# Attention values computed transposed in a hybrid decoder trunk on one core

## The chip, the core and the metric

The kernel runs on one core of one Trainium2 chip. The metric is the device time of one execution in microseconds (us); a comparison takes the median of several executions. The engines work in parallel, each through its own queue in order, and wait for each other through semaphores: TensorE (PE: matrix products, with weight loads PEld beside them), VectorE (DVE), ScalarE (ACT), GpSimd (POOL) and SyncE (SP), which here only issues transfers.

## What is computed

One layer on 256 tokens of width 1024, all in float32:

```
h = rmsnorm(x, g_mix);  proj = h @ w_in           # q, k, v (8 heads of 64), u, gate_a, gate_c
o = causal_softmax(q k^T / 8) v                   # one block of 256 keys: plain causal attention
branch_a = sigmoid(gate_a) * (o @ w_attn_up)
z = u_a * sigmoid(u_g);  z = causal depthwise conv(z, 31 taps) + b_dw
branch_c = sigmoid(gate_c) * (silu(layernorm(z)) @ w_conv_pw + b_conv_pw)
x = x + (branch_a + branch_c) @ w_out
x = x + relu(rmsnorm(x, g_ffn) @ w_ff1)^2 @ w_ff2
out = rmsnorm(x, g_final)
```

## The kernel before

**Products.** Weights arrive in units of 512 x 512 (1 MB). A unit goes through one of four slots: SP loads it into `raw`, ACT casts it to a high part `w_hi` (`high(n)`), DVE subtracts to get the low part `w_lo` (`low(n)`), and PE makes, for 2 token tiles and 4 row chunks, three products: high weights with low activations, high with high, low with high (`products`, L797), 24 in all, each 512 columns wide. The low and high parts of unit n + 3 are made while unit n runs (`AHEAD`). Units 0 to 17 are `w_in`, 18 and 19 `w_attn_up`, 20 and 21 `w_conv_pw`, then `w_out` and the MLP, which ends in a loop.

**Order.** Everything is written out by hand: one loop `for n in range(...)` per engine, in which the step of unit n is followed by what else the engine does "in slot n". Semaphores tie the engines.

**Attention.** Four pairs p of two heads. In slot 9 + p PE makes the scores of pair p (`scores`, L854), for the second 128 queries against 256 keys and for the first 128 against 128 keys, and adds the causal mask by a product of the identity with `mask_b`, as wide as the scores. The scores go to banks 6 and 7 (`SB0`), one bank per head. DVE takes the row maxima (`row_max`), ACT the exponentials with their row sums (`exps`) into `probs`. In slot 10 + p PE transposes the six 128 x 128 blocks (`probs_transposed`) into banks 4 and 5 (`TB`), and ACT copies them to `probs_t` (`probs_out`). In slot 11 + p PE multiplies them, as stationary operand, with the value rows (`values`), 64 columns per product, into columns 384 to 511 of the score banks; DVE multiplies by the inverse row sums (`inverse`, `o_out`) into `o_nat`. The order on PE in a slot is: unit, values, transposes, scores; and `scores(p)` waits for `o_out(p - 2)` (`o_made`). In slot 15 (`S_OT`) PE transposes `o_nat` by eight blocks, ACT and DVE split the result into `b_hi` and `b_lo`, the operand of unit 18.

**Beside it.** DVE makes the convolution in slots 2 to 14 (`conv_products`), one instruction of 256 columns per tap and channel chunk, 124 in all; `CONV_AT` says how many in which slot. ACT evicts every pair of units from PSUM (`take`), with a sigmoid for the gates; a change between Exp and Sigmoid costs a table load. In slot 13 (`S_BIAS`) it casts the bias rows, from which POOL takes the low part.

Of the kernel before, what the change touches and what calls it, by code (L numbers as in the profile page):

```python
# [48 lines left out]
S_OT = S_ATT + 6  # L49
# [5 lines left out]
CONV = [(tap, c) for tap in range(10) for c in (0, 1)]  # L55
CONV += [(tap, c) for tap in range(10) for c in (2, 3)]
CONV += [(tap, c) for tap in range(10, TAPS) for c in range(4)]
CONV_AT = {2: 6, 3: 14, 4: 9, 5: 9, 6: 9, 7: 9, 8: 9, 9: 10, 10: 10, 11: 10, 12: 10, 13: 10, 14: 9}
assert len(CONV) == sum(CONV_AT.values()) == TAPS * 4

# [18 lines left out]
def conv_before(m):  # L79

    tap, c = CONV[m]
    return CONV.index((tap - 1, c))


def build(nc, x, g_mix, w_in, b_glu, w_dw, b_dw, ln_g, ln_b, w_conv_pw, b_conv_pw,
# [35 lines left out]
    with ExitStack() as ctx:  # L121
# [23 lines left out]
        o_nat = sb("o_nat", [P, TT, A])  # L145
# [27 lines left out]
        gmix_rows = o_nat[0:KD, 0, 2 * P:3 * P]  # L173
        vec_rows = o_nat[0:VROWS, 0, 0:P]
        dw_rows = o_nat[0:TAPS * CC, 1, 0:P]
# [13 lines left out]
        def tile_chunks(bank, t):  # L189

            return ps[:, bank + t, :].rearrange("p (c t) -> p c t", c=4)

# [32 lines left out]
        z_made = sem("z_made")  # L225
        conv_step = sem("conv_step")
# [19 lines left out]
        o_made = sem("o_made")  # L246
        o_tr = sem("o_tr")
# [37 lines left out]
        def _(sp):  # L285
# [16 lines left out]
            for n in range(1, U_LOOP):  # L302
                if n // 2 <= UG:
                    load_halves(n, slice(0, HK), raw_full[n])
                else:
                    load(n, unit_source(n))
                if n == 1:
                    for row, v in ((V_BGLU, b_glu), (V_BDW, b_dw), (V_LNG, ln_g), (V_LNB, ln_b), (V_GFFN, g_ffn)):
                        rows = v.shape[1] // P
                        sp.dma_start(o_nat[row:row + rows, 0, 0:P], v.rearrange("l (c p) -> (l c) p", p=P)).then_inc(vec_full, 16)  # L310
# [65 lines left out]
        def _(act):  # L376
# [63 lines left out]

            def probs_out(p):
# [6 lines left out]
            for n in range(U_LOOP):  # L448
# [6 lines left out]
                if n in GLU_AT:  # L455
                    act.wait_ge(vec_made, 1)
                    for c in (2 * GLU_AT[n], 2 * GLU_AT[n] + 1):
                        act.wait_ge(glu_tr, c + 1)
                        nc.scalar.activation(conv[:, c], ps[:, TB + c, T:2 * T], ACT.Sigmoid,
                                             bias=vec[:, V_BGLU + CC + c:V_BGLU + CC + c + 1]).then_inc(glu_sig, 1)  # L460
                if n == S_QT:
                    qk_out(0, TB)
# [5 lines left out]
                if n < U_ATTN and n % 2 == 1 and n // 2 < GA:  # L468
                    take(n // 2)
                if S_ATT + 1 <= n <= S_ATT + PAIRS:  # L470
                    probs_out(n - S_ATT - 1)
                if S_ATT <= n < S_ATT + PAIRS:
                    exps(n - S_ATT)
                if n == S_ATT + PAIRS - 1:
# [3 lines left out]
                if n == S_OT:  # L478
                    act.wait_ge(o_tr, 1)
                    nc.scalar.copy(b_hi[:, 0:CC], chunks(TB)).then_inc(o_hi, 1)  # L480
# [73 lines left out]
        def _(dve):  # L554
# [31 lines left out]
            def conv_products(step):  # L586

                for m in conv_share(step):
                    tap, c = CONV[m]
                    if tap == 0:  # L590
                        nc.vector.tensor_scalar(conv[:, c], z[:, c, 0:T], dw[:, c:c + 1], vec[:, V_BDW + c:V_BDW + c + 1],
                                                ALU.mult, ALU.add).then_inc(conv_step, 1)
                    else:
                        dve.wait_ge(conv_step, conv_before(m) + 1)
                        w = tap * CC + c
                        nc.vector.scalar_tensor_tensor(out=conv[:, c], in0=z[:, c, tap:tap + T], scalar=dw[:, w:w + 1],  # L596
                                                       in1=conv[:, c], op0=ALU.mult, op1=ALU.add).then_inc(conv_step, 1)
# [14 lines left out]

            def o_out(p):

                dve.wait_ge(pv_done, p + 1)
                dve.wait_ge(rinv_made, p + 1)
                for s in range(2):
                    last = nc.vector.tensor_tensor(
                        o_nat[:, 1 - s, 128 * p:128 * p + 128].rearrange("p (h d) -> p h d", h=2),
                        ps[:, SB0:SB0 + 2, 384 + HD * s:384 + HD * s + HD],  # L620
                        rinv[:, p, 2 * s:2 * s + 2].rearrange("p (h a) -> p h a", a=1).to_broadcast([P, 2, HD]), ALU.mult)
                last.then_inc(o_made, 1)
# [8 lines left out]
            for n in range(U_LOOP):  # L631
# [10 lines left out]
                if S_ATT + 2 <= n < S_ATT + 2 + PAIRS:  # L642
                    o_out(n - S_ATT - 2)
                if S_ATT + 1 <= n < S_ATT + 1 + PAIRS:
                    inverse(n - S_ATT - 1)
                if S_ATT <= n < S_ATT + PAIRS:
                    row_max(n - S_ATT)
                if n == S_OT:
                    dve.wait_ge(o_hi, 1)
                    nc.vector.tensor_tensor(b_lo[:, 0:CC], chunks(TB), b_hi[:, 0:CC].bitcast(F32),  # L650
                                            ALU.subtract).then_inc(o_lo, 1)
# [81 lines left out]
                if n + AHEAD < U_LOOP + AHEAD_LOOP:  # L733
                    low(n + AHEAD)
                conv_products(n)

# [49 lines left out]
        def _(pe):  # L786
# [67 lines left out]
            def scores(p):  # L854

                if p >= 2:
                    pe.wait_ge(o_made, p - 1)
                for s, at, keys in ((1, 0, 256), (0, 256, 128)):  # L860
# [4 lines left out]
                    for h in range(2):  # L865
                        last = nc.tensor.matmul(ps[:, SB0 + h, at:at + keys], ident_b[:], mask_b[:, T - keys:T],  # L866
# [3 lines left out]
            def probs_transposed(p):  # L870
                pe.wait_ge(exp_made, p + 1)
                if p:
                    pe.wait_ge(pt_made, p)
                for blk in range(6):
                    o = blk * P
                    last = transpose(ps[:, TB + o // W, o % W:o % W + P], probs[:, o:o + P])
                last.then_inc(p_tr, 1)

            def values(p):

                pe.wait_ge(pt_made, p + 1)
                if p:
                    pe.wait_ge(o_made, p)
                if p + 2 <= PAIRS:
                    pe.wait_ge(exp_made, p + 2)
                for s in range(2):
                    for h in range(2):
                        head = slice(HD * (2 * p + h), HD * (2 * p + h) + HD)
                        o = 384 + HD * s
                        n_keys = 2 - s  # L890
                        for kb in range(n_keys):
                            at = 256 * h + P * kb if s == 0 else 512 + P * h
                            last = nc.tensor.matmul(ps[:, SB0 + h, o:o + HD], probs_t[:, at:at + P], v_nat[:, kb, head],  # L893
                                                    start=kb == 0, stop=kb == n_keys - 1)
# [12 lines left out]
            for n in range(1, U_ATTN):  # L907
# [22 lines left out]
                if S_ATT + 1 <= n <= S_ATT + PAIRS:  # L930
                    probs_transposed(n - S_ATT - 1)
                if S_ATT <= n < S_ATT + PAIRS:
                    if n == S_ATT:
                        pe.wait_ge(qk_made, 2)
                        pe.wait_ge(ident_made, 3)
                    scores(n - S_ATT)
                if n == S_OT:
                    pe.wait_ge(o_made, PAIRS)
                    transpose_chunks(TB, lambda t, c: o_nat[:, t, c * P:c * P + P]).then_inc(o_tr, 1)
                if n == S_LN:  # L940

                    pe.wait_ge(conv_step, TAPS * CC)
                    pe.wait_ge(o_lo, 1)
# [125 lines left out]
```

## Time and profile before

| | us |
|---|---|
| median of 3 executions | 367.96 |
| lowest, highest | 367.62, 368.09 |
| the profiled execution | 368.44 |
| its span, first to last instruction | 366.5 |
| PE busy in the span | 355.6 (97%) |
| DVE, ACT, POOL busy | 245.8, 174.9, 9.2 |

The profile is one execution of the same program. Durations of PE's matmuls overlap, since they are pipelined: what one costs in a stream is the distance between two starts, not its own length. In a timeline, consecutive instructions of a kind are one row with their count; an fp32 product is recorded as two passes, so that six products are x12. In brackets stand an engine's idle time before an instruction and the instruction that released it.

### The profile page before, as it was taken

The page shows a single profiled execution, that of the slowest core. Times are in us where ns is not written, and L with a number is a line of the kernel's source. Part 1 is how long each engine was busy: PE and PEld are TensorE (multiplying, and loading weights), DVE is VectorE, ACT ScalarE, POOL GpSimd, SP SyncE. Part 2 cuts the span into 40 slices and gives each one's busy share as a digit, 9 for nine tenths or more (in the row PEclk, how much of TensorE's full clock was granted, in tenths as well). Part 3 has the DMA queues.
Part 4 walks back from the last instruction along what each step waited for, and adds up shares of the span by engine and source line. Part 5 has one row for each costly group of instructions (what it writes and reads, how often), then busy time and mean ns, then how long its engine had stood idle before and what let it go on. Part 6 is the DMA issues. An engine that isn't in the chain of part 4 may idle for free.

```text
span 366.5 us, 5099 instructions
## 1 busy us (share of the span) xinstructions
PE 355.6 (97%) x2019; PEld 306.7 (84%) x2020; DVE 245.8 (67%) x298; ACT 174.9 (48%) x195; POOL 9.2 (3%) x18
## 2 busy tenths in 40 slices
PE   6999999999999999999999999999999999999993
PEld 3778888777788888888999899898998989989882
DVE  1779999898899779983837561736626375362734
ACT  3694454564493555353635643436344263541513
POOL 3000000000021000000000000000000000000000
PEclk9899999999999999999999999999999999999998
DMA  8998465533334563756364493671837628360003
GB/s 274 348 341 309 120 224 156 190 116 114 116 114 119 196 236 104 257 190 219 116 220 127 128 324 121 201 256 32 313 114 220 238 73 274 111 229 0 0 0 114
DMA packets 33993, 63.71 MB, mean 174 GB/s; under 512 B 1178, under 2 KB 5434, under 8 KB 33980
## 3 DMA queue, kind: packets, MB, share of 16 engines
q1 hardware_dynamic: 33676, 63.01, 51.7%
q10 hardware_dynamic: 304, 0.53, 0.4%
q8 instruction: 9, 0.15, 0.2%
q14 instruction: 4, 0.03, 0.0%
HBM read 62.48 MB, written 1.05 MB: 173 GB/s over the span
## 4 chain that ended last, share of the span: by engine, by line
PE 90%; DVE 5%; issue 2%; DMA 2%; ACT 0%; SPq 0%; POOLq 0%; POOL 0%
PE ps L805 20%; PE ps L801 20%; PE ps L802 19%; PE ps L1001 8%; PE ps L1002 8%; PE ps L1003 8%; PE ps L788 3%; DVE conv L596 2%; DMA raw<-in_w_in_dram 2%; DVE w_lo L558 1%; PE ps L863 1%; PE ps L893 1%; PE ps L866 1%; DVE smax L602 0%; DVE w_lo L575 0%
## 5 line engine op out<-in xcount | busy, mean ns | idle before, releaser
L801 PE MATMUL ps<-w_hi,a_lo 128*128 128x512 f32 x288 | 114.3, 397 | 2.5 <-DVE a_lo L570 2.5
L805 PE MATMUL ps<-w_lo,a_hi 128*128 128x512 f32 x288 | 113.0, 392 | 0.3 <-DVE w_lo L575 0.3
L802 PE MATMUL ps<-w_hi,a_hi 128*128 128x512 f32 x288 | 112.8, 392 | 0.0
L1001 PE MATMUL ps<-b_lo,w_hi 128*128 128x256 f32 x256 | 72.6, 284 | 0.0
L1002 PE MATMUL ps<-b_hi,w_hi 128*128 128x256 f32 x256 | 72.4, 283 | 0.0
L1003 PE MATMUL ps<-b_hi,w_lo 128*128 128x256 f32 x256 | 72.4, 283 | 0.0
L385 ACT CAST w_hi<-raw 128x2048 fp32r<-128x2048 f32 (+1 forms) x30 | 56.4, 1884 | 30.8 <-PE ps L805 26.5
L754 DVE TENSOR_TENSOR w_lo<-raw,w_hi 128x2048 fp32r<-128x2048 f32 x28 | 63.5, 2290 | 11.1 <-ACT w_hi L532 11.1
L558 DVE TENSOR_TENSOR w_lo<-raw,w_hi 128x2048 fp32r<-128x2048 f32 x29 | 66.0, 2282 | 5.1 <-ACT w_hi L385 5.0
L801 PEld LDWEIGHTS ps<-w_hi,a_lo 128*128 128x128 f32 x288 | 54.6, 190 | 13.3 <-DVE w_hi L564 2.7
L805 PEld LDWEIGHTS ps<-w_lo,a_hi 128*128 128x128 f32 x288 | 54.4, 189 | 12.3 <-DVE w_lo L575 0.8
L802 PEld LDWEIGHTS ps<-w_hi,a_hi 128*128 128x128 f32 x288 | 54.6, 190 | 10.6
L532 ACT CAST w_hi<-raw 128x2048 fp32r<-128x2048 f32 x28 | 52.7, 1910 | 7.5 <-PE ps L805 7.5
L596 DVE SCALAR_TENSOR_TENSOR conv<-z,dw,conv 128x256 f32<-128x256 f32 x120 | 50.7, 492 | 0.0
L1001 PEld LDWEIGHTS ps<-b_lo,w_hi 128*128 128x128 f32 x256 | 49.1, 192 | 0.6 <-ACT nat L516 0.3
L1002 PEld LDWEIGHTS ps<-b_hi,w_hi 128*128 128x128 f32 x256 | 49.1, 192 | 0.3
L1003 PEld LDWEIGHTS ps<-b_hi,w_lo 128*128 128x128 f32 x256 | 49.1, 192 | 0.0
L741 DVE TENSOR_TENSOR nat<-nat 128x1024 f32<-128x1024 f32 x7 | 8.6, 1225 | 46.4 <-ACT nat L516 46.4
L516 ACT ACTIVATE nat<-ps 128x512 f32<-128x512 f32 x16 | 9.6, 598 | 60.4 <-PE ps L1003 60.4
L801 PE MATMUL ps<-w_hi,b_lo 128*128 128x512 f32 x48 | 18.9, 393 | 0.0
L805 PE MATMUL ps<-w_lo,b_hi 128*128 128x512 f32 x48 | 18.7, 390 | 0.0
L802 PE MATMUL ps<-w_hi,b_hi 128*128 128x512 f32 x48 | 18.7, 389 | 0.0
(113 smaller groups left out, 227.1 us busy)
## 6 DMA issues: line engine op xcount, KB each, us to landing
raw<-in_w_ff_dram SPq DMA_DIRECT2D x32, 1024.0 KB, 5.5
raw<-in_w_in_dram SPq DMA_DIRECT2D x14, 1024.0 KB, 5.2
raw<-in_w_out_dram SPq DMA_DIRECT2D x4, 1024.0 KB, 5.1
raw<-in_w_in_dram SPq DMA_DIRECT2D x6, 512.0 KB, 7.8
raw<-in_w_attn_up_dram SPq DMA_DIRECT2D x2, 1024.0 KB, 5.0
raw<-in_w_conv_pw_dram SPq DMA_DIRECT2D x2, 1024.0 KB, 5.0
res<-in_x_dram SPq DMA_DIRECT2D x2, 512.0 KB, 3.8
raw<-in_w_in_dram SPq DMA_DIRECT2D x4, 256.0 KB, 5.6
```

The costliest lines, as they stand in the source:

```text
L385: nc.scalar.copy(w_hi[:, n % SLOTS, part], raw[:, n % SLOTS, part]).then_inc(hi_made, 1)
L532: nc.scalar.copy(w_hi[:, slot], raw[:, slot]).then_inc(hi_made, 1)
L558: nc.vector.tensor_tensor(w_lo[:, n % SLOTS], raw[:, n % SLOTS], w_hi[:, n % SLOTS].bitcast(F32), ALU.subtract).then_inc(lo_made, 1)
L596: nc.vector.scalar_tensor_tensor(out=conv[:, c], in0=z[:, c, tap:tap + T], scalar=dw[:, w:w + 1], in1=conv[:, c], op0=ALU.mult, op1=ALU.ad ...
L754: nc.vector.tensor_tensor(w_lo[:, slot], raw[:, slot], w_hi[:, slot].bitcast(F32), ALU.subtract).then_inc(lo_made, 1)
L788: return nc.tensor.transpose(dst, src, ident[0:src.shape[0], 0:src.shape[0]])
L801: nc.tensor.matmul(dst, lo[:, tok], w_hi[:, slot, k], start=start, stop=False)
L802: nc.tensor.matmul(dst, hi[:, tok], w_hi[:, slot, k], start=False, stop=False)
L805: return nc.tensor.matmul(dst, hi[:, tok], w_lo[:, slot, k], start=False, stop=stop)
L1001: nc.tensor.matmul(dst, w_hi[:, slot, k, cols], b_lo[:, kk], start=kk == 0, stop=False)
L1002: nc.tensor.matmul(dst, w_hi[:, slot, k, cols], b_hi[:, kk], start=False, stop=False)
L1003: last = nc.tensor.matmul(dst, w_lo[:, slot, k, cols], b_hi[:, kk], start=False, stop=kk == KD - 1)
```

## The change

Value rows become the stationary operand and the transposed probabilities move. The product then comes out transposed, so that the output transposes of slot 15 are gone. The inverse row sums can no longer be applied to the output (they would run along its columns), so ACT scales `probs` before they are transposed (`normalise`). In detail:

- `values(p)`: four products with 64 stationary columns, of 256, 256, 128 and 128 moving columns; the two heads write the lower and the upper 64 partitions of one piece of bank 5 (`o_pair`).
- `o_out(p)` moves from DVE to ACT, as a copy of 256 columns to `o_t`, in ACT's slot 11 + p ahead of `probs_out`.
- `scores(p)` comes ahead of `probs_transposed(p - 1)` in a slot and waits for `exp_made` of the pair before.
- `probs_transposed(p)` waits for `norm_made` and for `ot_made` of the pair before.
- `inverse(p)` moves a slot earlier on DVE, behind `low(n + 3)`.
- The masks are 128 columns wide throughout.
- Tap 0 of the convolution, with the bias, moves to ACT in slots 2 and 4; DVE is left with 120 instructions.

```
             def normalise(p):
+                act.wait_ge(rinv_made, p + 1)
+                act.wait_ge(exp_made, p + 1)
+                for h in range(2):
+                    part = probs[:, 256 * h:256 * h + 256]
+                    nc.scalar.activation(part, part, ACT.Copy, scale=rinv[:, p, h:h + 1])
+                for h in range(2):
+                    part = probs[:, 512 + 128 * h:640 + 128 * h]
+                    last = nc.scalar.activation(part, part, ACT.Copy, scale=rinv[:, p, 2 + h:3 + h])
+                last.then_inc(norm_made, 1)
+            def o_out(p):
+                act.wait_ge(pv_done, p + 1)
+                nc.scalar.copy(o_t[:, p], o_pair()).then_inc(ot_made, 1)
...
+                    for c in (2 * GLU_AT[n], 2 * GLU_AT[n] + 1):
+                        act.wait_ge(z_made, c + 1)
+                        nc.scalar.activation(conv[:, c], z[:, c, 0:T], ACT.Identity, scale=dw[:, c:c + 1],
+                                             bias=vec[:, V_BDW + c:V_BDW + c + 1]).then_inc(conv_first, 1)
...
             def scores(p):
-                if p >= 2:
-                    pe.wait_ge(o_made, p - 1)
...
-                        last = nc.tensor.matmul(ps[:, SB0 + h, at:at + keys], ident_b[:], mask_b[:, T - keys:T],
+                        last = nc.tensor.matmul(ps[:, SB0 + h, at + keys - P:at + keys], ident_b[:], mask_b[:, P:T],
                                                 start=False, stop=True)
             def probs_transposed(p):
-                pe.wait_ge(exp_made, p + 1)
+                pe.wait_ge(norm_made, p + 1)
                 if p:
                     pe.wait_ge(pt_made, p)
+                    pe.wait_ge(ot_made, p)
...
             def values(p):
                 pe.wait_ge(pt_made, p + 1)
                 if p:
-                    pe.wait_ge(o_made, p)
-                if p + 2 <= PAIRS:
-                    pe.wait_ge(exp_made, p + 2)
+                    pe.wait_ge(ot_made, p)
+                for kb in range(2):
                     for h in range(2):
                         head = slice(HD * (2 * p + h), HD * (2 * p + h) + HD)
+                        at = 3 * h * P + 2 * P * kb
+                        last = nc.tensor.matmul(o_pair()[HD * h:HD * h + HD, kb * P:T], v_nat[:, kb, head],
+                                                probs_t[:, at:at + T - kb * P], start=kb == 0, stop=kb == 1)
```

PE, slot 11, between the last product of unit 11 and the first of unit 12. `v_nat` and `probs_t` are values and transposed probabilities, `qk_t` the queries and keys. Before:

```order
L805 MATMUL ps<-w_lo,a_hi 128x512
L893 MATMUL ps<-v_nat,probs_t 128x64 x6
L788 MATMUL ps<-ident,probs 128x128 x6
L863 MATMUL ps<-qk_t 128x256 x2
L866 MATMUL ps<-mask_b,ident_b 128x256 x2
L863 MATMUL ps<-qk_t 128x128 x2
L866 MATMUL ps<-mask_b,ident_b 128x128 x2
L801 MATMUL ps<-w_hi,a_lo 128x512
```

Now:

```order
L822 MATMUL ps<-w_lo,a_hi 128x512
L903 MATMUL ps<-probs_t,v_nat 64x256 x2
L903 MATMUL ps<-probs_t,v_nat 64x128 x2
L876 MATMUL ps<-qk_t 128x256 x2
L879 MATMUL ps<-mask_b,ident_b 128x128 x2
L876 MATMUL ps<-qk_t 128x128 x2
L879 MATMUL ps<-mask_b,ident_b 128x128 x2
L805 MATMUL ps<-ident,probs 128x128 x6
L818 MATMUL ps<-w_hi,a_lo 128x512
```

The transposes of the probabilities have moved behind the scores, and the values are four products instead of six.

PE, slot 13, where there are no scores any more; the brackets name what an instruction waits for. Now:

```order
L822 MATMUL ps<-w_lo,a_hi 128x512
L903 MATMUL ps<-probs_t,v_nat 64x256 [waits ot_made,pt_made]
L903 MATMUL ps<-probs_t,v_nat 64x256
L903 MATMUL ps<-probs_t,v_nat 64x128 x2
L805 MATMUL ps<-ident,probs 128x128 [waits ot_made,pt_made,norm_made]
L805 MATMUL ps<-ident,probs 128x128 x5
L818 MATMUL ps<-w_hi,a_lo 128x512 [waits lo_made,hi_made,evac]
```

The transposes stand straight behind the values, and wait for ACT's copy of these values' result; before, they waited for `pt_made` and `exp_made`.

ACT, from the end of slot 12 into slot 13: exponentials of pair 3, a table load with the gates of unit pair 5, the high part of unit 16, the bias rows. Before:

```order
L446 COPY probs_t<-ps 128x768
L433 ACTIVATE probs,psums<-ps,nbias 128x256 x2
L436 ACTIVATE probs,psums<-ps,nbias 128x128 x2
L422 ACT_TABLE_LOAD
L422 ACTIVATE gates<-ps,rstd 128x512 x2
L385 CAST w_hi<-raw 128x2048
L467 CAST bias_rows<-gfin_bc 128x1024
L446 COPY probs_t<-ps 128x768
L422 ACTIVATE gates<-ps,rstd 128x512 x2
```

Now:

```order
L468 COPY probs_t<-ps 128x768
L438 ACTIVATE probs,psums<-ps,nbias 128x256 x2
L441 ACTIVATE probs,psums<-ps,nbias 128x128 x2
L452 ACTIVATE probs<-probs,rinv 128x256 x2
L455 ACTIVATE probs<-probs,rinv 128x128 x2
L427 ACT_TABLE_LOAD
L427 ACTIVATE gates<-ps,rstd 128x512 x2
L390 CAST w_hi<-raw 128x2048
L495 CAST bias_rows<-gfin_bc 128x1024
L461 COPY o_t<-ps 128x256
L468 COPY probs_t<-ps 128x768
L427 ACTIVATE gates<-ps,rstd 128x512 x2
```

The four scalings (L452, L455) stand behind the exponentials, and the copy of the output (L461) behind the bias cast.

## Rows read from the trace of the kernel before

**Rows 1.** The page's first part, and the head of its fourth, by engine.

```profile
PE 355.6 (97%) x2019; PEld 306.7 (84%) x2020; DVE 245.8 (67%) x298; ACT 174.9 (48%) x195; POOL 9.2 (3%) x18
...
PE 90%; DVE 5%; issue 2%; DMA 2%; ACT 0%; SPq 0%; POOLq 0%; POOL 0%
```

**Rows 2.** Timeline of PE, slots 10 and 11: start, us, engine, line, tiles.

```profile
77.39 0.82 PE L788 MATMUL ps<-ident,probs 128*128 128x128 f32 x6
78.13 0.70 PE L863 MATMUL ps<-qk_t 64*128 64x256 f32 x4
...
86.45 0.82 PE L788 MATMUL ps<-ident,probs 128*128 128x128 f32 x6
87.67 0.70 PE L863 MATMUL ps<-qk_t 64*128 64x256 f32 x4 [0.39 <-DVE o_nat L618]
88.30 0.39 PE L866 MATMUL ps<-mask_b,ident_b 128*128 128x256 bf16 x2
88.62 0.49 PE L863 MATMUL ps<-qk_t 64*128 64x128 f32 x4
89.05 0.29 PE L866 MATMUL ps<-mask_b,ident_b 128*128 128x128 bf16 x2
```

**Rows 3.** Timeline of PE, slots 12 to 15.

```profile
98.68 0.48 PE L801 MATMUL ps<-w_hi,a_lo 128*128 128x512 f32 x1
...
104.22 1.45 PE L893 MATMUL ps<-v_nat,probs_t 128*128 128x64 f32 x12
105.50 0.83 PE L788 MATMUL ps<-ident,probs 128*128 128x128 f32 x6
...
118.47 1.04 PE L788 MATMUL ps<-ident,o_nat 128*128 128x128 f32 x8
119.26 0.47 PE L801 MATMUL ps<-w_hi,a_lo 128*128 128x512 f32 x1
```

**Rows 4.** Groups by line and shape: busy us, mean ns of one.

```profile
L397 ACT ACTIVATE a_hi<-ps,gmix 128x256 fp32r<-128x256 f32 x8 | 3.1, 474 | 1.1 <-PE ps L788 1.1
```

**Rows 5.** Timeline of DVE, slot 12.

```profile
98.91 0.69 DVE L602 TENSOR_REDUCE smax<-ps 128x2 f32<-128x512 f32 x1 [1.68 <-PE ps L866]
...
99.96 0.17 DVE L607 TENSOR_SCALAR nbias<-smax 128x4 f32<-128x4 f32 x1
100.04 2.28 DVE L558 TENSOR_TENSOR w_lo<-raw,w_hi 128x2048 fp32r<-128x2048 f32 x1
102.24 4.04 DVE L596 SCALAR_TENSOR_TENSOR conv<-z,dw,conv 128x256 f32<-128x256 f32 x10
```

**Rows 6.** Timeline of ACT, slots 12 and 13.

```profile
100.17 0.48 ACT L433 ACTIVATE probs<-ps,nbias 128x256 f32<-128x256 f32 x1 [2.54 <-DVE nbias L607]
100.54 0.19 ACT L433 ACTIVATION_READ_ACCUMULATOR probs<-ps,nbias 128x1 f32 x1
...
101.90 1.28 ACT L422 ACT_TABLE_LOAD   x1
103.20 1.27 ACT L422 ACTIVATE gates<-ps,rstd 128x512 f32<-128x512 f32 x2
104.36 1.90 ACT L385 CAST w_hi<-raw 128x2048 fp32r<-128x2048 f32 x1
106.15 1.05 ACT L467 CAST bias_rows<-gfin_bc 128x1024 fp32r<-128x1024 f32 x1
107.10 0.80 ACT L446 COPY probs_t<-ps 128x768 f32<-128x768 f32 x1
```

**Rows 7.** PE near the start, then a stretch (its third number from the end: granted clock).

```profile
9.44 0.47 PE L801 MATMUL ps<-w_hi,a_lo 128*128 128x512 f32 x1 [2.48 <-DVE a_lo L570]
...
11.28 0.62 PE L805 MATMUL ps<-w_lo,a_hi 128*128 128x512 f32 x1
...
14.68 0.40 PE L802 MATMUL ps<-w_hi,a_hi 128*128 128x512 f32 x1
...
11.27:14.69 3.42, 3.42 (x10) 2.65 (x9) 2.94 (x6) 2.43 (x3) 0.00 (x0) 0.50 1.11 335
```

**Rows 8.** Timeline of ACT, slot 4 into slot 5.

```profile
41.52 1.92 ACT L385 CAST w_hi<-raw 128x2048 fp32r<-128x2048 f32 x1 [2.31 <-PE ps L805]
```

More of the change, by code:

```diff
@@ L52 @@
 S_SILU = U_ATTN
-CONV = [(tap, c) for tap in range(10) for c in (0, 1)]
-CONV += [(tap, c) for tap in range(10) for c in (2, 3)]
+CONV = [(tap, c) for tap in range(1, 10) for c in (0, 1)]
+CONV += [(tap, c) for tap in range(1, 10) for c in (2, 3)]
 CONV += [(tap, c) for tap in range(10, TAPS) for c in range(4)]
-CONV_AT = {2: 6, 3: 14, 4: 9, 5: 9, 6: 9, 7: 9, 8: 9, 9: 10, 10: 10, 11: 10, 12: 10, 13: 10, 14: 9}
-assert len(CONV) == sum(CONV_AT.values()) == TAPS * 4
+CONV_AT = {2: 6, 3: 12, 4: 9, 5: 9, 6: 9, 7: 9, 8: 9, 9: 10, 10: 10, 11: 10, 12: 10, 13: 9, 14: 8}
+assert len(CONV) == sum(CONV_AT.values()) == (TAPS - 1) * 4
 F32 = mybir.dt.float32
@@ L144, in build @@
         probs_t = sb("probs_t", [P, 768])
[L145 removed]
+        o_t = sb("o_t", [P, CC, T])
         PAD = TAPS - 1
@@ L245, in build @@
         rinv_made = sem("rinv_made")
-        o_made = sem("o_made")
-        o_tr = sem("o_tr")
+        norm_made = sem("norm_made")
+        ot_made = sem("ot_made")
         o_hi = sem("o_hi")
@@ L309, in _ @@
                         rows = v.shape[1] // P
-                        sp.dma_start(o_nat[row:row + rows, 0, 0:P], v.rearrange("l (c p) -> (l c) p", p=P)).then_inc(vec_full, 16)
+                        sp.dma_start(o_t[row:row + rows, 0, 0:P], v.rearrange("l (c p) -> (l c) p", p=P)).then_inc(vec_full, 16)
                     sp.dma_start(dw_rows, w_dw.rearrange("l j (c p) -> (l j c) p", p=P)).then_inc(vec_full, 16)
@@ L469, in _ @@
                     take(n // 2)
+                if S_ATT + 2 <= n < S_ATT + 2 + PAIRS:
+                    o_out(n - S_ATT - 2)
                 if S_ATT + 1 <= n <= S_ATT + PAIRS:
@@ L477, in _ @@
                     take(n // 2)
-                if n == S_OT:
-                    act.wait_ge(o_tr, 1)
-                    nc.scalar.copy(b_hi[:, 0:CC], chunks(TB)).then_inc(o_hi, 1)
+                if n == S_OLO:
+                    act.wait_ge(ot_made, PAIRS)
+                    nc.scalar.copy(b_hi[:, 0:CC], o_t[:]).then_inc(o_hi, 1)
                 if n == S_SILU:
@@ L611, in inverse @@
                 nc.vector.reciprocal(rinv[:, p], psums[:, p]).then_inc(rinv_made, 1)
[L613 to L622, printed above, removed]
             def tile_products(n, t):
@@ L734, in _ @@
                     low(n + AHEAD)
+                if S_ATT <= n < S_ATT + PAIRS:
+                    inverse(n - S_ATT)
                 conv_products(n)
+                if n == S_OLO:
+                    dve.wait_ge(o_hi, 1)
+                    nc.vector.tensor_tensor(b_lo[:, 0:CC], o_t[:], b_hi[:, 0:CC].bitcast(F32),
+                                            ALU.subtract).then_inc(o_lo, 1)
             def hidden_square(blocks):
@@ L935, in _ @@
                         pe.wait_ge(ident_made, 3)
+                    else:
+                        pe.wait_ge(exp_made, n - S_ATT)
                     scores(n - S_ATT)
-                if n == S_OT:
-                    pe.wait_ge(o_made, PAIRS)
-                    transpose_chunks(TB, lambda t, c: o_nat[:, t, c * P:c * P + P]).then_inc(o_tr, 1)
+                if S_ATT + 1 <= n <= S_ATT + PAIRS:
+                    probs_transposed(n - S_ATT - 1)
                 if n == S_LN:
-                    pe.wait_ge(conv_step, TAPS * CC)
-                    pe.wait_ge(o_lo, 1)
+                    pe.wait_ge(conv_step, (TAPS - 1) * CC)
+                    pe.wait_ge(ot_made, PAIRS)
                     for t in range(TT):
```

52 lines of the change are left out of this document (21 added, 31 removed).

## The prediction

> **What bounds the kernel now.** I read the page's first and fourth part first. TensorE (PE) is busy 97% of the 366.5 us span, and the chain that ended last runs over PE for 90% [rows 1]. So an edit is worth what it takes from or puts between PE's instructions; VectorE (DVE, 67%) and ScalarE (ACT, 48%) matter only where PE waits for them. Then PE's timeline around the attention, and the two timelines of DVE and ACT beside it. Call "slot n" unit n's 24 products with the attention work behind them.
>
> In slots 11 and 12 the scores wait for DVE's `o_out`: from the start of six transposes to the start of the scores it takes 0.74 us where nothing is waited for (77.39 to 78.13) and 1.22 us where it is (86.45 to 87.67) [rows 2]. That is 0.48 us, twice.
>
> **The change part by part.** The profiled execution took 368.44 us, 0.48 above the median of the three runs (367.96); its span is 366.5. I make the sum in its times and put the difference on the median.
>
> *Masks.* Two of the four mask products of a pair shrink from 256 to 128 columns. A group of two takes 0.39 us at 256 and 0.29 at 128 [rows 2]: 0.10 a pair, 0.4 us in all, on PE's path.
>
> *Waits of the scores.* They wait no more for `o_made`, but for `exp_made` of the pair before, a slot old. 0.96 us go.
>
> *Values.* Before, 6 products of 64 moving columns (12 recorded passes) take 1.28 us, 104.22 to 105.50 [rows 3]. After, four products with 64 stationary columns: two move 256 columns, two 128. No row shows an fp32 product whose output is half the columns. The nearest are the score products, which use half the rows: a group of two heads takes 0.63 us at 256 moving columns and 0.42 at 128, with the other head's product beside it [rows 2]. By these the new values cost 1.05 us, 0.23 less. Upper bound: if the heads go one after the other, each group costs twice its streaming share. The two group times differ by 0.21 us for 128 columns, so streaming is 0.42 and 0.21 of them and the fixed rest 0.21; doubled, 1.05 and 0.63, together 1.7 us. Lower bound, the fixed rest paid only once: 0.85. I take 1.05, since the heads' overlap was seen on the same type and widths, and 0.1 more for the last pair, which now switches shape between two units. For four pairs: 0.8 us gained.
>
> The Trainium skill, "TensorEngine Tiling (Array Packing)", sections "Theoretical Speedup" and "Tiling Modes", says that half the columns give up to twice the speed, and that changing the mode drains the engine. By its factor the serial 1.7 would become 0.85 and the sum 0.6 us smaller; the score rows, with their fixed 0.21, argue against the full factor.
>
> *Output transposes.* Eight go from slot 15: 118.47 to 119.26 [rows 3], 0.8 us.
>
> These are 0.4 + 0.96 + 0.8 + 0.8 = 3.0 us gained on PE. (Of the values of pair 2 the gain lands ahead of the wait below, so that it only lengthens the wait; the sum comes out the same.)
>
> *Normalising on ACT and the output copy.* Now `o_out` and four scalings stand in ACT's queue, and `probs_transposed(p)` waits for `ot_made`, ACT's copy of the pair before. In slots 11 and 12 scores lie between the values and those transposes and cover the copy (about 0.5 us: a 256-column operation takes 0.47 [rows 4]). In slot 13 there are no scores. What ACT does ahead of `o_out(2)`, from R, the start of pair 3's row maximum on DVE:
> - the low part of the next weights stands ahead of `inverse` on DVE and ends at R + 3.33 (98.91 to 102.24) [rows 5]; the exponentials start at R + 1.26 and are over by R + 3.0 (100.17 to 101.90) [rows 6], so DVE's order decides;
> - `inverse` reaches ACT 0.20 later, as `nbias` does (99.96 to 100.17) [rows 5, 6]: R + 3.5;
> - four scalings: two of 256 columns at the exponentials' 0.37 (100.17 to 100.54) [rows 6], two of 128 at 0.25 (half of it and a fixed rest), and a tail of 0.1: R + 4.9. The nearest row is an ACTIVATE of 256 columns with a scale, 474 ns in full [rows 4]; 1.1 to 1.9 us are the bounds;
> - table load 1.30, gates 1.16, high part of the weights 1.79, bias cast 0.95 (from 101.90 to 107.10) [rows 6]: R + 10.1;
> - the copy, 0.5: R + 10.6.
>
> PE before starts unit 13 at 98.68 and row maximum 3 is at 98.91. After, 0.3 (three masks) + 0.96 + 0.46 come off ahead of it, and the maximum is also 0.66 earlier, since the transposes of pair 2 (0.66: the 0.74 above without the change of shape) now follow the scores. So unit 13 starts near 97.0, takes 5.54 (98.68 to 104.22) [rows 3] and its values 1.05: PE stands at 103.5. R is 98.91 - 1.72 - 0.66 = 96.5, and the copy lands at 107.1. **PE waits 3.6 us in slot 13**, where it waited for nothing. Behind it on PE stand the transposes, unit 14 and all the rest.
>
> 3.6 - 3.0 = +0.6 us.
>
> *What the wait does to the clock.* At the start PE idles 2.48 us, until 9.44, and from 11.27 its granted clock is 0.50 (1.2 of 2.4 GHz) for 3.42 us: eight products start in the 3.40 us from 11.28 to 14.68 [rows 7], 0.425 each against 5.54 / 24 = 0.23. That costs 8 x 0.195 = 1.6 us. The new idle stretch is longer than the one before that fall, though it has dense products on both sides. I take the fall as likelier than not: +0.6 + 1.6 = +2.2 us.
>
> The same ACT queue is where a page differs from the rows. The Trainium skill, "ScalarE: Activation LUTs", section "What ACT_TABLE_LOAD costs", gives 1.28 us for the load and 1.38 for a drain. Rows 6 have 1.30 from the load to the gates and no drain ahead of it; by the page the wait and the sum would be 1.4 us longer.
>
> *Edits with no effect on the end.* Tap 0 of the convolution goes from DVE to ACT, four operations of about 0.37 us. The second pair makes ACT wait for DVE's z, but ACT idled 2.31 us there, until 41.52 [rows 8]; if the cover is gone, the next high part of weights is some 0.6 us late, three units ahead of use. DVE loses 8 `o_out` operations, and its later low parts move by 1 to 3 us in slots 13 to 15, still units ahead of use. `norm_made` comes at R + 4.9, two us before the transposes.
>
> **The rivals.**
> - *The wait comes, the clock stays.* +0.6 us: 368.6. For it: the only fall recorded follows a stretch in which PE did transposes and then nothing, not dense products. Against: the gap is 3.6 us and not 2.5.
> - *The two heads don't overlap in column halves.* Values 1.7 instead of 1.05; three of four pairs count (pair 2's hides in the wait): +1.9 more, 370.5 without and 372.1 with the fall. For: no row shows column halves. Against: the row halves overlap.
> - *The other side: ACT is there in time.* If the copy came before PE needs it, the 3.0 us stand: 365.0. The point is 3.6 us off the 10.6 us chain, more than the scalings and the table load together (2.7). For: ACT has slack as a whole (48%), and a slip of mine in where `o_out` stands would do. Against: each link is an instruction in one queue with its row, and the queue's order puts gates, cast and bias cast ahead of the copy.
> - *The change doesn't do what it says*, that is, the scalings or casts bring further table loads: 1.3 us each in every slot. The order lists the same three loads, so I give it no chance of its own.
>
> **How the numbers follow.** Wait and fall 55%, 370.2; wait without fall 17%; heads in series 15%; ACT in time 8%; the rest 5%. The predicted time is 367.96 + 2.2 = 370.2. Bounds: the values from 0.85 to 1.7 give -0.6 to +1.9, the scalings -0.2 to +0.6, the fall 0 or 1.6. The range is 368.3 to 372.2: it holds the first two cases and most of the third. 0.2% is 0.74 us, about what a measurement of this kernel can tell from no change; the case without the fall lies at that edge and is split. Faster 0.08, same 0.10, slower 0.82.
>
> **What would show it.** Right: PE idle some 3.6 us before the first transposes of `probs` in slot 13 near 103.5 us, released by ACT's copy of `o_t`, with a granted clock of 0.50 for some 3.4 us in unit 14; no wait in slots 11 and 12; values near 1.05 us. Wrong: the copy landing before 103.5, values of 1.7 us, scalings far from 1.2 us for four, or new waits in slots 10 to 12 (then the scores or transposes came late for the exponentials, which by the same chain have about two us to spare).

## The result

| | before | after |
|---|---|---|
| median of 6 executions of each, us | 368.2 | 370.5 |
| lowest, highest | 367.6, 368.6 | 369.5, 371.3 |
| the profiled execution | 368.44 | 370.84 |
| its span | 366.5 | 369.0 |

The ratio of after to before is 1.0061, with a 95% interval from 1.0047 to 1.0076: the changed kernel is 2.3 us slower by the medians, 2.2 by the ratio. The forecast was +2.2 us, 370.2.

### The profile page after: what moved, and what is told of

Read it like the earlier page. It is cut to its first block, busy times and chain, and to the rows that moved or that the text cites. A ratio compares the mean times of both kernels' runs of the same rounds, so it can differ in the third digit from the quotient of the medians.

```text
span 369.0 us, 5065 instructions
## 1 busy us (share of the span) xinstructions
PE 354.6 (96%) x1995; PEld 303.3 (82%) x1996; DVE 243.0 (66%) x286; ACT 183.9 (50%) x219; POOL 8.8 (2%) x18
## 3 DMA queue, kind: packets, MB, share of 16 engines
HBM read 62.48 MB, written 1.05 MB: 172 GB/s over the span
## 4 chain that ended last, share of the span: by engine, by line
PE 89%; ACT 3%; DMA 2%; issue 2%; DVE 2%; SPq 1%; POOLq 0%; POOL 0%
PE ps L818 20%; PE ps L819 19%; PE ps L822 19%; PE ps L1010 8%; PE ps L1011 8%; PE ps L1012 8%; PE ps L805 3%; DMA raw<-in_w_in_dram 2%; DVE w_lo L589 1%; PE ps L876 1%; ACT w_hi L390 1%; PE ps L903 1%; SPq L300 1%; PE ps L879 0%; ACT L427 0%
```

## The profile after

The page's first part and the head of its fourth (the chain that ended last, by engine), as [rows 1] show them for before:

```profile
PE 354.6 (96%) x1995; PEld 303.3 (82%) x1996; DVE 243.0 (66%) x286; ACT 183.9 (50%) x219; POOL 8.8 (2%) x18
...
PE 89%; ACT 3%; DMA 2%; issue 2%; DVE 2%; SPq 1%; POOLq 0%; POOL 0%
```

PE has 24 instructions fewer and is busy 1.0 us less, and yet the span is 2.5 us longer; ACT, which had 0% of the chain, now has 3%. So the loss doesn't lie in more work for PE but in a wait for ACT and, as the rows below show, in a slower clock behind it. PE's timeline of slot 11 (start, us, engine, line, tiles), the counterpart of the second half of [rows 2]:

```profile
85.11 0.87 PE L903 MATMUL ps<-probs_t,v_nat 128*64 128x256 f32 x8
85.91 0.70 PE L876 MATMUL ps<-qk_t 64*128 64x256 f32 x4
86.54 0.29 PE L879 MATMUL ps<-mask_b,ident_b 128*128 128x128 bf16 x2
86.76 0.49 PE L876 MATMUL ps<-qk_t 64*128 64x128 f32 x4
87.18 0.29 PE L879 MATMUL ps<-mask_b,ident_b 128*128 128x128 bf16 x2
87.30 0.83 PE L805 MATMUL ps<-ident,probs 128*128 128x128 f32 x6
87.89 0.47 PE L818 MATMUL ps<-w_hi,a_lo 128*128 128x512 f32 x1
```

No row carries a wait. The values take 0.80 us (85.11 to 85.91) where they took 1.28, and the first mask group 0.22 (86.54 to 86.76) where it took 0.32. Slots 13 and 14, the counterpart of [rows 3]:

```profile
96.31 0.47 PE L818 MATMUL ps<-w_hi,a_lo 128*128 128x512 f32 x1
...
101.96 0.87 PE L903 MATMUL ps<-probs_t,v_nat 128*64 128x256 f32 x8
106.69 1.51 PE L805 MATMUL ps<-ident,probs 128*128 128x128 f32 x6 [3.87 <-ACT o_t L461]
107.86 0.78 PE L818 MATMUL ps<-w_hi,a_lo 128*128 128x512 f32 x1
...
115.52 0.87 PE L903 MATMUL ps<-probs_t,v_nat 128*64 128x256 f32 x8
116.32 0.50 PE L818 MATMUL ps<-w_hi,a_lo 128*128 128x512 f32 x1
```

PE stands still for 3.87 us ahead of the transposes of pair 3, until ACT's copy to `o_t`. Behind the gap everything is slow: six transposes take 1.17 us (106.69 to 107.86) instead of 0.58 (105.50 to 106.08 before), and unit 14 takes 7.66 (107.86 to 115.52) instead of 5.56 (106.08 to 111.64 before). The engines' busy time in three stretches, whose third number from the end is the granted clock of PE:

```profile
98.00:105.00 7.00, 4.83 (x26) 3.49 (x24) 5.37 (x12) 6.51 (x14) 0.00 (x0) 1.00 0.49 150
105.34:112.17 6.83, 5.47 (x16) 4.64 (x17) 6.80 (x8) 4.96 (x6) 3.52 (x1) 0.50 0.45 152
...
112.20:119.00 6.80, 6.80 (x35) 5.15 (x34) 6.80 (x13) 2.18 (x2) 0.00 (x0) 1.00 0.28 105
```

From 105.34, while PE still idled, to 112.17 the granted clock is 0.50, 1.2 of 2.4 GHz, and then 1.00 again. ACT's queue in slots 12 and 13 shows what the copy stood behind; [rows 6] are its counterpart:

```profile
99.47 0.91 ACT L452 ACTIVATE probs<-probs,rinv 128x256 f32<-128x256 f32 x2 [0.46 <-DVE rinv L641]
100.29 0.68 ACT L455 ACTIVATE probs<-probs,rinv 128x128 f32<-128x128 f32 x2
100.99 1.28 ACT L427 ACT_TABLE_LOAD   x1
102.28 1.26 ACT L427 ACTIVATE gates<-ps,rstd 128x512 f32<-128x512 f32 x2
103.44 1.90 ACT L390 CAST w_hi<-raw 128x2048 fp32r<-128x2048 f32 x1
105.22 1.05 ACT L495 CAST bias_rows<-gfin_bc 128x1024 fp32r<-128x1024 f32 x1
106.17 0.38 ACT L461 COPY o_t<-ps 128x256 f32<-128x256 f32 x1
```

The values are over at 102.8, but the copy starts at 106.17: four scalings, a table load, gates, a high part and the bias cast come first, without a gap.

The whole difference can be read from PE's starts (a unit's row runs from its own first product to that of the next unit, with the attention work between):

| from, to | before | after | difference |
|---|---|---|---|
| unit 9 to unit 11 | 14.89 | 14.63 | -0.26 |
| unit 11 to 12 | 9.53 | 8.41 | -1.12 |
| unit 12 to 13 | 9.54 | 8.42 | -1.12 |
| unit 13 to 14 | 7.40 | 11.55 | +4.15 |
| unit 14 to 15 | 6.81 | 8.46 | +1.65 |
| unit 15 to the convolution's transposes | 11.92 | 11.02 | -0.90 |

They sum to +2.40; unit 9 starts 0.13 later (64.85 against 64.72), which makes the 2.5 us of the spans.

## The experiments

My theory: the change frees some 3 to 4 us of PE and pays with a wait in slot 13, which comes from the place of `o_out(2)` in ACT's queue, and with a half clock that the wait brings. The rivals were that the half clock has another cause, that the order of scores and transposes costs or gives something of its own, that moving tap 0 had an effect of its own, and, for the values, that only neighbouring products of the two heads overlap, or that a pass with 64 output columns is simply shorter, whatever runs beside it. Each comparison has its own runs of the kernel before on the same chip: 368.05 us for the first four kernels, 368.43 for the next four, 368.21 for the last three.

**The copy first in its slot.** After, with ACT's copy of pair 2 ahead of the high part and the bias cast:

```
             for n in range(U_LOOP):
+                if n == S_BIAS:
+                    o_out(2)
                 if n + AHEAD < U_LOOP + AHEAD_LOOP:
...
-                if S_ATT + 2 <= n < S_ATT + 2 + PAIRS:
+                if S_ATT + 2 <= n < S_ATT + 2 + PAIRS and n != S_BIAS:
                     o_out(n - S_ATT - 2)
```

> The changed kernel with one edit: in slot 13 ACT copies pair 2's output ahead of the high part of unit 16 and of the bias cast. Theory W (PE waits in slot 13 for what stands ahead of the copy in ACT's queue, and this idle stretch halves the clock): 1.79 + 0.95 us leave the queue ahead of the copy, so PE's 3.9 us of idling become about 1.1, too short for the clock to fall; together 2.8 + 2.3 us less than the changed kernel: about 365.4, 2.8 under the kernel before. Theory S (the new product shapes bring the clock down, not the gap): the granted clock still falls after slot 13, and only the 2.8 us go: 367.7. Theory N (ACT's queue isn't what PE waits for): 370.5.

Measured: 365.93 us, ratio 0.9939 (0.9916 to 0.9962). PE's timeline of this kernel in slot 13:

```profile
104.22 0.85 PE L807 MATMUL ps<-ident,probs 128*128 128x128 f32 x6 [1.12 <-ACT o_t L461]
104.83 0.48 PE L820 MATMUL ps<-w_hi,a_lo 128*128 128x512 f32 x1
```

One copy moved ahead of two instructions, and the wait shrinks from 3.87 to 1.12 us; the transposes take 0.61 us (104.22 to 104.83), so at the full clock. Together that is 4.6 us less than after, more than the 2.75 of the wait alone; 365.4 was expected.

**No wait at all.** After, with the output of pair 2 in free columns of the score banks, so that the transposes of pair 3 need not wait for its copy, which ACT makes from there (not shown). The piece is 128 columns wide in each bank, so that the four products become six:

```
                     pe.wait_ge(pt_made, p)
-                    pe.wait_ge(ot_made, p)
+                    pe.wait_ge(ot_made, min(p, 2))
...
+                if p == 2:
+                    pe.wait_ge(exp_made, PAIRS)
+                    for half, kb in ((0, 0), (1, 0), (1, 1)):
+                        for h in range(2):
+                            head = slice(HD * (2 * p + h), HD * (2 * p + h) + HD)
+                            at = (3 * h + half + kb) * P
+                            last = nc.tensor.matmul(ps[HD * h:HD * h + HD, SB0 + half, 3 * P:4 * P], v_nat[:, kb, head],
+                                                    probs_t[:, at:at + P], start=kb == 0, stop=kb == half)
+                    last.then_inc(pv_done, 1)
+                    return
```

> The changed kernel, with pair 2's output written to the free columns of the two score banks, by six products of 128 columns instead of four, so that the transposes of pair 3 need not wait for ACT's copy. ACT's queue is untouched. Theory W: PE's wait in slot 13 goes altogether, and the clock stays whole: 3.9 + 2.3 us less, some 0.1 more for the extra products: 364.4. Theory S: the wait goes, the clock still falls somewhere near 105 us: 366.7. Theory N: the delay of ACT's queue comes back at the next thing that PE needs from it (pair 3's copied probabilities in slot 14): above 367.

Measured: 364.18 us, ratio 0.9894 (0.9878 to 0.9911), 1.1% faster than before. Slot 13 on its PE:

```profile
101.72 0.88 PE L909 MATMUL ps<-probs_t,v_nat 128*64 128x128 f32 x12
102.52 0.88 PE L809 MATMUL ps<-ident,probs 128*128 128x128 f32 x6
103.36 0.50 PE L822 MATMUL ps<-w_hi,a_lo 128*128 128x512 f32 x1
```

ACT's copy is as late as ever, and nobody waits for it:

```profile
102.04 1.27 ACT L427 ACTIVATE gates<-ps,rstd 128x512 f32<-128x512 f32 x2
...
105.93 0.38 ACT L462 COPY o_t<-ps 128x256 f32<-128x256 f32 x1
```

So the gain is real and was given back in one place. The next limit is already there: six transposes need 0.58 us, but unit 14 starts 0.84 after their start, at 103.36, right behind the gates' end (103.31). The gates free the banks into which unit 14 writes.

**The wait filled.** After, with 16 products of zeros between values and transposes of slot 13. PE still waits for the copy, but is busy while it does:

```
+                if n == S_BIAS:
+                    pe.wait_ge(exp_made, PAIRS)
+                    for _ in range(16):
+                        nc.tensor.matmul(ps[:, SB0], zero_b[:, 0:P], zero_b[:], start=True, stop=True)
                 if S_ATT + 1 <= n <= S_ATT + PAIRS:
```

> The changed kernel, with 16 products of zeros (128x512, into a free score bank) on PE between pair 2's values and the transposes of pair 3, so that PE is busy while it would wait; the result doesn't use them. 16 x 0.227 = 3.6 us fit into the wait of 3.9. Theory W: the transposes start when they did, since ACT's copy sets that, but the clock doesn't fall: 2.3 us less, 368.2, like the kernel before. Theory S: the clock falls as before, 370.5. If the wait isn't ACT's, the products add themselves: 374.

Measured: 367.97 us, ratio 0.9998 (0.9988 to 1.0007). PE's timeline, and the stretch in which after had the half clock:

```profile
102.41 3.63 PE L950 MATMUL ps<-zero_b 128*128 128x512 bf16 x16
106.35 0.85 PE L805 MATMUL ps<-ident,probs 128*128 128x128 f32 x6 [0.31 <-ACT o_t L461]
106.95 0.47 PE L818 MATMUL ps<-w_hi,a_lo 128*128 128x512 f32 x1
```

```profile
105.34:112.17 6.83, 6.52 (x33) 5.06 (x31) 6.83 (x9) 4.63 (x6) 3.56 (x1) 1.00 0.48 154
```

The copy lands as late as in after (this execution runs 0.35 us ahead of it: its values of slot 11 start at 84.76 against 85.11), DMA, DVE, ACT and POOL do nearly the same, and the clock stays at 1.00. So PE's idleness brings the fall, not the time or the other engines, and the fall costs 370.5 - 368.0 = 2.5 us, or 2.3 if each kernel is compared with its own runs of before. This splits the loss: about 3.8 us for the wait (368.0 - 364.2) and 2.3 to 2.5 for the clock.

**The wait alone, in the kernel before.** Its values of slot 13 wait for ACT's bias cast:

```
+                    if n == S_BIAS:
+                        pe.wait_ge(bias_hi, 1)
                     values(n - S_ATT - 2)
```

> The kernel before, with one wait more on PE: in slot 13, ahead of the values of pair 2, it waits for the bias cast on ACT, which ends near 107.2 us while PE is there at 104.2. Nothing of the new shapes or order is in it. Theory W: PE idles 3.0 us and the clock falls afterwards: 368.2 + 3.0 + 1.6 to 2.3 = 373. Theory S: only the 3.0 us, 371.2.

Measured: 373.67 us, ratio 1.0145 (1.012 to 1.017). Its PE, and a stretch behind the wait:

```profile
107.33 2.71 PE L893 MATMUL ps<-v_nat,probs_t 128*128 128x64 f32 x12 [2.88 <-ACT bias_rows L467]
109.83 1.49 PE L788 MATMUL ps<-ident,probs 128*128 128x128 f32 x6
110.97 0.78 PE L801 MATMUL ps<-w_hi,a_lo 128*128 128x512 f32 x1
```

```profile
107.49:114.30 6.81, 6.81 (x26) 6.13 (x27) 4.22 (x8) 2.94 (x4) 2.22 (x1) 0.50 0.10 5
```

A wait of 2.88 us costs 5.6: the values behind it take 2.50 us (107.33 to 109.83) instead of 1.28, and the granted clock is 0.50 from 107.49 to 114.30. None of the change's other parts is in this kernel, so the fall needs none of them. The four executions lie between 372.6 and 374.9 us, and the rows are those of the longest, so they show the fall at its dearest; the other three were not read in their rows.

**The bias cast elsewhere.** After, with the cast and its POOL work two slots later, which takes 0.95 us out of the chain ahead of the copy:

```
-S_BIAS = 13
+S_BIAS = 15
```

> The changed kernel, with the cast of the bias rows on ACT (0.95 us) in slot 15 instead of 13, so that the copy of pair 2's output comes that much sooner. Theory W: PE's idle stretch in slot 13 shrinks from 3.9 to 2.9 us. Where the clock still falls, 0.95 us less: 369.5; where it doesn't, 0.95 + 2.3 us less: 367.2. The kernel before with an added wait of 2.9 us showed a fall, so 369.5 is expected. Theory N (something else than the queue ahead of the copy sets the wait): 370.5.

Measured: 368.76 us, ratio 1.0009 (0.9988 to 1.0031), but ten executions lie between 366.43 and 369.93, where the kernel before stays within 1.6 us in nineteen. The profiled one took 367.0:

```profile
105.25 0.85 PE L805 MATMUL ps<-ident,probs 128*128 128x128 f32 x6 [2.92 <-ACT o_t L461]
105.86 0.47 PE L818 MATMUL ps<-w_hi,a_lo 128*128 128x512 f32 x1
```

The wait is 2.92 us as the chain says, and here no half clock follows it (0.61 us for the transposes). The mean granted clock of the ten goes from 0.998 in the shortest two (366.4, 367.0; 0.997 and 0.998) down to 0.985 in the longest (369.9), with exceptions between. The likely reading is that a wait of this length brings the clock down in some executions and not in others. Only one was read in its rows, so that is argued from the mean clocks and not shown; in the kernel before with a wait of 2.88 us the fall was there. The mean clock alone doesn't tell where a fall lies: before, with no wait in slot 13, has means from 0.990 to 0.999 as well, for there is another fall near the start in some executions (last section).

The other kernels start from the version without the wait (364.2 us).

**Order of scores and transposes.** The transposes ahead of the scores again, as in the kernel before:

```
                     values(n - S_ATT - 2)
+                if S_ATT + 1 <= n <= S_ATT + PAIRS:
+                    probs_transposed(n - S_ATT - 1)
                 if S_ATT <= n < S_ATT + PAIRS:
...
                     scores(n - S_ATT)
-                if S_ATT + 1 <= n <= S_ATT + PAIRS:
-                    probs_transposed(n - S_ATT - 1)
```

> The kernel of e2_other_banks (364.2 us), with the transposes of the probabilities ahead of the scores again in every slot. Theory: in slots 11 and 12 the transposes then wait for ACT's copy of the values' result, which needs some 0.55 us after the values, with nothing between: 1.1 us in all, 365.3. The scores ahead of the transposes are worth that. Rival (the order doesn't matter, the copy hides in PE's own latency): 364.2.

Measured: 367.44 us, ratio 0.9971 (0.9961 to 0.998): about 3 us slower than with the new order (3.2 by the medians, 2.9 by the spans of the profiled executions), where 1.1 were expected. Its PE in slots 11 and 13, then ACT in slot 11:

```profile
84.85 0.87 PE L917 MATMUL ps<-probs_t,v_nat 128*64 128x256 f32 x8
86.67 0.85 PE L809 MATMUL ps<-ident,probs 128*128 128x128 f32 x6 [0.94 <-ACT o_t L465]
...
104.86 0.87 PE L809 MATMUL ps<-ident,probs 128*128 128x128 f32 x6
106.32 0.50 PE L822 MATMUL ps<-w_hi,a_lo 128*128 128x512 f32 x1 [0.58 <-ACT gates L427]
```

```profile
84.37 1.89 ACT L390 CAST w_hi<-raw 128x2048 fp32r<-128x2048 f32 x1
86.17 0.36 ACT L465 COPY o_t<-ps 128x256 f32<-128x256 f32 x1
```

The values end at 85.65, and the copy starts 0.5 us later, at 86.17, since a high part stands ahead of it in every slot. I had counted only the copy. Slots 11 and 12 become 1.2 us longer each. The third part is in slot 13: the transposes start at 104.86 and unit 14 only at 106.32, when the gates are through, 1.46 us later, where it was 0.84 above. I had left out those 0.6 us. So the new order is the part without which the rest would gain only 1 us.

**Tap 0 back on DVE** (and out of ACT's queue, which isn't shown):

```
+                    if tap == 0:
+                        nc.vector.tensor_scalar(conv[:, c], z[:, c, 0:T], dw[:, c:c + 1], vec[:, V_BDW + c:V_BDW + c + 1],
+                                                ALU.mult, ALU.add).then_inc(conv_step, 1)
```

> The kernel of e2_other_banks (364.2 us), with tap 0 of the convolution back on DVE (four instructions more there, four less on ACT). Theory: no effect on the end, since neither engine is waited for there: 364.2. Rival (DVE's queue is so full up to slot 9 that its 1.6 us reach PE through the low parts of the weights or the row maxima): up to 365.8.

Measured: 364.29 us, ratio 0.9892 (0.9873 to 0.9912), against 364.18 and 0.9894 with tap 0 on ACT. No effect is seen.

**Wide masks.** The masks of the second queries 256 columns wide again, in one execution:

```
-                        last = nc.tensor.matmul(ps[:, SB0 + h, at + keys - P:at + keys], ident_b[:], mask_b[:, P:T],
+                        last = nc.tensor.matmul(ps[:, SB0 + h, at:at + keys], ident_b[:], mask_b[:, T - keys:T],
```

> The kernel of e2_other_banks (364.2 us), with the masks of the second 128 queries 256 columns wide again. Expected: 0.10 us more in each of four pairs on PE, 364.6, seen in the distance of the rows and hardly in the time.

Measured: 364.85 us in one run, which alone says little. The rows do:

```profile
86.44 0.39 PE L883 MATMUL ps<-mask_b,ident_b 128*128 128x256 bf16 x2
86.77 0.49 PE L880 MATMUL ps<-qk_t 64*128 64x128 f32 x4
```

0.33 us instead of 0.22, so 0.11 a pair.

**Why the values cost 0.80.** I had forecast 1.05 from the two heads' overlap. First, the heads one after the other in program order (here and in the next two, pair 2's six products are changed in the same way, which isn't shown):

```
-                for kb in range(2):
-                    for h in range(2):
+                for h in range(2):
+                    for kb in range(2):
```

> The kernel of e2_other_banks (364.2 us), with the products of the values ordered head by head (both key blocks of one head, then of the other) instead of alternating between the heads. Nothing else differs. Theory C (the 0.80 us of a pair, against a streaming time of 1.28 for its eight passes one after the other, come from two column halves that work side by side, and only neighbours of different heads can): a pair takes 1.3 to 1.5 us, 0.5 to 0.7 more each: 366.2 to 367.0. Rival (the passes are shorter with 64 output columns, whatever stands beside them): 364.2.

Measured: 364.4 us, ratio 0.9893 (0.9867 to 0.9919), and 0.81 us a pair. In its trace the passes start in pairs 13 ns apart, as if the two heads stood side by side. My theory that only neighbours overlap fell for these four products. It didn't fall altogether: pair 2 has six products of 128 columns, and head by head they take 1.07 us in this kernel's slot 13,

```profile
101.76 1.15 PE L909 MATMUL ps<-probs_t,v_nat 128*64 128x128 f32 x12
102.83 0.87 PE L809 MATMUL ps<-ident,probs 128*128 128x128 f32 x6
```

where they took 0.80 alternating (101.72 to 102.52, above). So with six passes to a head the order costs 0.27 us; the wait for the gates behind them nearly hides it (unit 14 starts at 103.46, against 103.36).

Then the products of one head alone:

```
-                    for h in range(2):
+                    for h in range(1):
```

> The kernel of e2_other_banks (364.2 us), with the values' products of the second head of each pair left out, so that half of the attention output is stale data: half the passes. Theory C (the two column halves work side by side): the other head's passes cost nothing, a pair still takes 0.80 us, 364.2. Rival (a pass with 64 output columns is simply shorter and they run one after the other): half of 0.80, 0.4 us less in each of four pairs, 362.6.

Measured: 364.06 us, ratio 0.9888 (0.9858 to 0.9918).

```profile
84.25 0.86 PE L917 MATMUL ps<-probs_t,v_nat 128*64 128x256 f32 x4
85.05 0.70 PE L880 MATMUL ps<-qk_t 64*128 64x256 f32 x4
```

Half the passes, and the same 0.80 us: the second head is free, and the rival (0.40 us a pair) falls. Last, the kernel with the heads in turn, with both on the same 64 output partitions:

```
-                        last = nc.tensor.matmul(o_pair()[HD * h:HD * h + HD, kb * P:T], v_nat[:, kb, head],
+                        last = nc.tensor.matmul(o_pair()[0:HD, kb * P:T], v_nat[:, kb, head],
```

> The kernel of e6_heads_in_turn (364.4 us), with both heads' products written to the same 64 output partitions, so that they use the same column half of the array (the second head overwrites the first, the output is wrong there). Same instructions, widths and order otherwise. Theory C: the passes now run one after the other, 4 x 0.213 + 4 x 0.107 = 1.28 us of streaming and 0.1 to 0.4 of weight loads: 1.4 to 1.7 instead of 0.80 us, 366.8 to 368.0. Rival (shorter passes, one after the other in either case): 364.4.

Measured: 366.35 us, ratio 0.9947 (0.9928 to 0.9966).

```profile
84.41 1.51 PE L917 MATMUL ps<-probs_t,v_nat 128*64 128x256 f32 x8
85.86 0.70 PE L880 MATMUL ps<-qk_t 64*128 64x256 f32 x4
```

1.45 us instead of 0.81, from nothing but the output's place. The time is lower than the 366.8 to 368.0 expected, in part since some 0.27 us fall into slot 13's wait for the gates. One head's streaming is then 1.45 - 0.80 = 0.65 us and the fixed rest 0.15, and the two heads run beside each other because they write different halves of the columns. The Trainium skill, "TensorEngine Tiling (Array Packing)", section "Theoretical Speedup", gives up to twice the speed for a small side of 64 or less. Here it was 1.45 / 0.80 = 1.8, on the part that streams the full two.

## Why the prediction was right, point by point

The mechanism was the one forecast: a wait for ACT's copy in slot 13, and a half clock behind it. The total is within 0.3 us, but that it is so near is luck, since it hides two terms that were both too small and cancel.

- *Masks*: 0.10 a pair forecast, 0.10 in after's rows, 0.11 with the edit undone. Right.
- *Waits of the scores*: both gone; slots 11 and 12 are 1.12 shorter each, of which values are 0.48 and masks 0.10, so 0.54 is left where 0.48 was forecast. Right.
- *Output transposes*: 0.8 forecast, slot 15 is 0.90 shorter. Right.
- *Values*: **mis-sized.** I took 1.05 from the score products with their fixed rest of 0.21 per group, and named 0.85, with that rest paid once, as the lower bound. Measured 0.80: four pairs took 5.1 us and take 3.2, so they gain 1.9 instead of 0.8. The overlap was there, but the fixed rest was charged twice, and the 0.1 for the last pair's change of shape doesn't show (0.80 there too, 115.52 to 116.32). The step that argued "the score rows, with their fixed 0.21, argue against the full factor" was the wrong choice between row and page: the page's factor was nearer.
- *The wait*: 3.6 forecast, 3.87 measured. ACT's chain was right to 0.2 us: R is 95.93, and the copy starts at R + 10.24 where R + 10.1 was forecast. The scalings take 1.5 us from 99.47 to 100.99 where 1.4 was taken. The rest of the difference is PE, whose values take 0.25 us less than forecast; it is as the prediction said, pair 2's gain only lengthens the wait. The drain of 1.38 us ahead of a table load (the Trainium skill, "ScalarE: Activation LUTs", section "What ACT_TABLE_LOAD costs") isn't in the rows: the load at 100.99 follows right behind the last scaling, and the gates start 1.29 us after it.
- *The clock*: the fall came, as forecast at better than even odds, **but was mis-sized**. I took its length, 3.4 us, from the only one in the trace of before [rows 7]; it lasted 6.83, which is twice that. Read from the starts it costs 0.6 on the transposes and 2.1 on unit 14, 2.7 in all against 1.6 forecast; filling the wait gives 2.3 to 2.5. With its first part in the idle stretch, only some 5.5 of the 6.83 us held work.
- *The sum*: gained 0.26 + 1.12 + 1.12 + 0.90, and the values of pairs 2 and 3 in slots 13 and 14, 0.48 + 0.45: 4.3 us, 3.0 forecast. Paid 3.9 + 2.7 = 6.6 with 0.2 unassigned, 5.2 forecast. Two terms that were each 1.1 us short, one of gain and one of loss, gave the right total.
- *The rivals*: "the wait comes, the clock stays" is what filling the wait makes, 368.0 against the 368.6 that I gave. "ACT is there in time" is the version without the wait: 364.2 against 365.0, low by the values' term. "The heads don't overlap" is wrong; its 1.7 us a pair would be 1.45. "Further table loads" did not come.
- *Tap 0 and `norm_made`*: no effect, as said. The high part behind tap 0 is 0.6 us late, as forecast (42.14 against 41.52 in [rows 8]), and nobody waits for it.

## What to carry to other kernels

When work moves to an engine with slack, read what stands ahead of it in that engine's queue in the one slot where the cover is thinnest: this change gains 4 us over slots 9 to 15 and loses 6.6 behind the one place where the transposes follow the values with no scores between. A wait of some 3 us or more on TensorE can cost more than half of itself again, or nearly all, through the clock (2.5 on 3.87, 2.7 on 2.88). Where it can't be avoided, 16 products of zeros in it won back 2.5 us though the wait stayed as long; one copy moved up in ACT's queue took 4.6 us for 2.75 us less of waiting. Check a right total term by term: this one was right because two errors had the same size.

## What the hardware showed beside this

- Two fp32 products of 64 stationary columns whose outputs lie in different 64-partition halves cost what one costs (0.80 us with four or eight passes); in the same half they take 1.45. Head by head in program order that still held for four passes to a head (0.81), and only in part for six (1.07 against 0.80).
- The half clock lasted 3.42 us in one stretch [rows 7] and 6.8 in slot 13, in two kernels. There it followed idle stretches of 3.87 and 2.88 us, and not one of 1.12; behind 2.92 it was absent in the one execution whose rows were read. In the first it began in the idle stretch, 2.5 us after PE's last product; in the second 0.16 us behind its end.
- Near the start, three of the thirteen profiled executions have a half clock of 3.42 us: before, with the copy first, and with no wait. PE had idled 2.48, 2.83 and 2.50 us there; in the other ten, after among them (1.76), it idled 1.42 to 2.29 and the clock stayed. That fall costs little. After has none, and there PE waits for DVE's low part instead:

```profile
16.95 0.47 PE L818 MATMUL ps<-w_hi,a_lo 128*128 128x512 f32 x1 [1.09 <-DVE w_lo L589]
```

  Before has no such wait, and its next transposes (of `nat`) start at 25.84, in after at 25.97. The 1.6 us that the prediction read from [rows 7] are thus what eight products cost, and reach the total only where PE is what everything waits for, as in slots 13 and 14.
- POOL's addition on one partition (`bias_rows`, 3.5 to 3.9 us) holds up one instruction of DVE's convolution beside it. DVE's timeline in after, then POOL's:

```profile
107.58 5.76 DVE L626 SCALAR_TENSOR_TENSOR conv<-z,dw,conv 128x256 f32<-128x256 f32 x9
```

```profile
106.35 3.52 POOL L372 TENSOR_TENSOR bias_rows<-gfin_bc,bias_rows 1x1024 fp32r<-1x1024 f32 x1 [84.36 <-ACT bias_rows L495]
```

Nine taps take 5.76 us, where ten take 4.04 in [rows 5]. In both kernels the first of them has some 2.1 us more than the others (2.59 us in after and 2.64 in before, instead of 0.48), and it ends 0.3 us after POOL's instruction does. The kernel with the bias cast two slots later ties this to the bias work; there POOL adds from 115.63, and the same nine taps are even:

```profile
107.08 3.64 DVE L626 SCALAR_TENSOR_TENSOR conv<-z,dw,conv 128x256 f32<-128x256 f32 x9
```

POOL in turn seems to wait for DVE: its instruction ends 2.2 to 2.3 us after the end of the low part that DVE makes beside it, in all three kernels. That is read from the coincidence alone. No engine waits for either here.
